# When the residual x and the small tables are loaded, and when the combinations of x are made

## The reference

```python
def swiglu(x, w_gate, w_up, w_down):
    return (jax.nn.silu(x @ w_gate) * (x @ w_up)) @ w_down

x = layer_norm(ALPHA * x + 0.5 * swiglu(x, ffn_w_gate[l, 0], ffn_w_up[l, 0], ffn_w_down[l, 0]), ln_g[l, 0], ln_b[l, 0])
```

## Time and profile before

| what | value |
|---|---|
| median of the runs | 1128.38 us (1127.18 to 1129.8) |
| the profiled execution's own time | 1126.32 us |
| its span, first to last instruction | 1124.3 us |
| PE busy | 1114.1 us, 99% |
| DVE busy | 776.9 us, 69% |
| ACT busy | 531.9 us, 47% |
| mean granted clock of PE | 0.999 |

### The profile page before, as it was taken

The page is one execution under the profiler, slowest core; times in us unless marked ns, Lnnn a source line. Parts: engine busy times, 40 slices in busy tenths (PEclk is TensorE's granted clock), DMA queues, the critical chain, the costliest instruction groups (busy, mean ns, idle before and its releaser), DMA issues.

```text
span 1124.3 us, 17750 instructions
## 1 busy us (share of the span) xinstructions
PE 1114.1 (99%) x6752; PEld 992.1 (88%) x6752; DVE 776.9 (69%) x1274; ACT 531.9 (47%) x913; POOL 35.5 (3%) x51
## 2 busy tenths in 40 slices
PE   9999999999999999999999999999999999999997
PEld 7899999988888888888898888889899999998886
DVE  4998898753338588774894865557898888863326
ACT  4555555543325477643463453436355555552222
POOL 2000000000002011000000000000000000000000
PEclk9999999999999999999999999999999999999999
DMA  8533333363222222342243242231233333353301
GB/s 286 201 113 113 107 101 111 96 211 94 94 75 89 80 77 84 104 150 75 75 157 126 88 156 75 73 97 58 75 127 99 113 113 96 113 185 99 108 21 75
DMA packets 34121, 123.37 MB, mean 110 GB/s; under 512 B 3916, under 2 KB 3932, under 8 KB 33792
## 3 DMA queue, kind: packets, MB, share of 16 engines
q1 hardware_dynamic: 30528, 109.07, 30.3%
q0 software_dynamic: 3520, 13.29, 3.5%
HBM read 120.23 MB, written 2.11 MB: 109 GB/s over the span
## 4 chain that ended last, share of the span: by engine, by line
PE 94%; DVE 3%; DMA 2%; ACT 1%; issue 0%; DVEq 0%; SPq 0%
PE ps L515 19%; PE ps L516 19%; PE ps L517 19%; PE ps L593 10%; PE ps L594 10%; PE ps L595 10%; DMA raw<-in_units 2%; PE ps L817 1%; PE ps L532 1%; PE ps L796 1%; PE ps L884 1%; PE ps L868 1%; PE ps L789 0%; PE ps L788 0%; PE ps L980 0%
## 5 line engine op out<-in xcount | busy, mean ns | idle before, releaser
L1572 DVE TENSOR_TENSOR wlo<-raw,whi 128x1024 fp32r<-128x1024 f32 x124 | 151.8, 1230 | 171.8 <-ACT whi L1046 170.8
L1046 ACT ACTIVATE whi<-raw 128x1024 fp32r<-128x1024 f32 (+1 forms) x131 | 134.4, 1033 | 135.3 <-PE ps L517 124.2
L515 PE MATMUL ps<-whi,hhi 128*128 128x512 f32 x480 | 187.9, 391 | 0.0
L517 PE MATMUL ps<-whi,hlo 128*128 128x512 f32 x480 | 186.9, 389 | 0.0
L516 PE MATMUL ps<-wlo,hhi 128*128 128x512 f32 x480 | 186.8, 389 | 0.0
L515 PE MATMUL ps<-xth,whi 128*128 128x512 f32 (+1 forms) x340 | 129.6, 381 | 0.0
L517 PE MATMUL ps<-xth,wlo 128*128 128x512 f32 (+1 forms) x340 | 127.5, 375 | 0.0
L516 PE MATMUL ps<-xtl,whi 128*128 128x512 f32 (+1 forms) x340 | 127.4, 375 | 0.0
L517 PEld LDWEIGHTS ps<-whi,hlo 128*128 128x128 f32 x480 | 90.1, 188 | 19.0
L515 PEld LDWEIGHTS ps<-whi,hhi 128*128 128x128 f32 x480 | 90.1, 188 | 18.5 <-ACT km L1046 0.3
L516 PEld LDWEIGHTS ps<-wlo,hhi 128*128 128x128 f32 x480 | 90.2, 188 | 17.9
(11 more groups left out here) (258 smaller groups left out, 2639.1 us busy)
## 6 DMA issues: line engine op xcount, KB each, us to landing
raw<-in_units SPq DMA_DIRECT2D x204, 512.0 KB, 3.5
xraw<-in_units POOLq DMA_DIRECT2D x1, 2048.0 KB, 13.3
xn<-in_x POOLq DMA_DIRECT2D x4, 512.0 KB, 15.2
gb<-in_ln_g POOLq DMA_DIRECT2D x4, 512.0 KB, 3.8
gb<-in_ln_b POOLq DMA_DIRECT2D x4, 512.0 KB, 5.3
wb<-in_bias_by_key POOLq DMA_DIRECT2D x8, 256.0 KB, 3.0
out<-xn SPq DMA_DIRECT2D x8, 256.0 KB, 2.1
gsp<-g_rows POOLq DMA_DIRECT2D x1, 1024.0 KB, 5.1
```

Source lines behind the costliest of these rows:

```text
L515: mm(dst, lh, rh, start=start, stop=False)
L517: return mm(dst, ll, rh, start=False, stop=stop)
L1046: return nc.scalar.activation(*a, **k)
L1572: v.tensor_tensor(wlo[c % SPL][:, :], raw[c % RAW][:, :], whi[c % SPL][:, :].bitcast(F32), ALU.subtract).then_inc(lo_done, 1)
```

## The change

On POOL a wait for `unit_used` is put between the load of `xraw` and the small tables. Its value is 4 + 8 + 2 = 14, which is reached when PE has done all of tile 4, `part4` included. On DVE and on ACT, for the first block alone (n is 0), tile 1 comes behind the combinations of x and not ahead of them.

```diff
--- before.py
+++ after.py
@@ -438,6 +438,7 @@
 
             pool.wait_ge(lo_done, KT - 2)
             pool.dma_start(xraw[0][:, :, :], units[0:KT, :, 0:S].rearrange("k p c -> p k c")).then_inc(xraw_in, 16)
+            pool.wait_ge(unit_used, U_F1 + 2 * FAST0 + 2)
             pool.dma_start(ccol[:, :], conv_cols).then_inc(small_in, 16)
             pool.dma_start(lnm_sb[:, :], lnm).then_inc(small_in, 16)
             pool.dma_start(gbias[:, 0:1], ig_bias.rearrange("a h -> h a")).then_inc(small_in, 16)
@@ -1163,10 +1164,13 @@
                         split(u0 + 2 * f + AHEAD + 1)
 
                 tile(0)
-                tile(1)
+                if n:
+                    tile(1)
                 for j, (x, rows, cols) in enumerate(((x5, high, far), (x7, low, far), (x6, low, near), (x3, high, near))):
                     act.wait_ge(xs_done, 4 * n + j + 1)
                     fn(x[n][0][:, :, :], xraw[n][:, rows, cols], ACT.Copy).then_inc(xc_hi_done, 1)
+                if n == 0:
+                    tile(1)
                 tile(2)
                 both, sums, last = fast_hi(n, FAST0)
                 both()
```

## The result

The changed kernel takes 1131.12 us (median of 12 runs, 1130.15 to 1132.52), the kernel before 1128.37 us (12 runs, 1127.01 to 1130.1). The ratio is 1.0024, with a 95% interval of 1.0016 to 1.0033: slower by 2.7 us, 1.8 to 3.7. The profiled execution took 1131.89 us, with a span of 1129.9 us and a mean granted clock of 0.997.

A forecast was written before the change was run, and what follows sets the result against it. PE was taken as the bound, busy 99%. A stop of 4.17 us and 0.1, less 1.96 regained, gave +2.3 us; on the median of 1128.38 that is 1130.7 us, range 1128.7 to 1134.3.

The forecast's parts named there:

- The stop at unit 10: Before tile 3 PE waits for unit 10's low part, behind the combinations on DVE: 4.17 us lost.
- What goes in return: PE's two waits in tile 4 (0.96 and 0.80 us) and their slow restarts go: 1.96 us back.
- The clock: At PE's stop before tile 3 the granted clock stays up; rival: it falls, +2.0 us, to 1132.7, chance 0.16.
- I am wrong if [...] the clock falls: Sign against the forecast: the granted clock, expected at 1.00 through 38 to 50 us, falls.
- The sum: By the start of tile 5: +4.17 + 0.1 - 1.96 = +2.3 us, which stays to the end.
- chance of 0.62 for slower: Chance that the whole kernel comes out slower by more than the 0.2% bound, 2.26 us; same 0.34, faster 0.04.
- Unit 11's low part: On DVE ahead of tile 3's second unit: 1.14 us later, still 5.4 us before PE wants it.
- The residual and the tables: Loads moved behind tile 4: put at 0, bounds 0 and +2.0 us; rival, they collide with weight loads, chance 0.10.
- the room that was worked out: In the fast tiles a weight load 2.0 us late would fit within 2.3 us of room before PE waits.
- The other side: Rival: not slower, the stop before tile 3 is worth less than the two waits removed; down to 1126.4, chance 0.08.

The follow-up runs named there:

- order alone: The changed kernel without POOL's wait, so residual and tables load as in the kernel before: 1130.56 us, ratio 1.0025 to the kernel before.
- splits first: The changed kernel with the high and low parts of units 10 and 11 ahead of the combinations: 1127.48 us, ratio 0.9996 to the kernel before.
- unit 10 in the middle: The changed kernel with unit 10's low part between the second and third low part of the combinations: 1127.67 us, ratio 0.9998 to the kernel before.
- short fill: The changed kernel with 8 identity matmuls into an unused bank where PE waits for unit 10: 1130.94 us, ratio 1.0025 to the kernel before.
- long fill: The changed kernel with 16 identity matmuls into an unused bank where PE waits for unit 10: 1129.45 us, ratio 1.0015 to the kernel before.
- unit 9 split early: The kernel before with late loads and ACT's high part of unit 9 ahead of its wait for the opening's end: 1126.65 us, ratio 0.9987.

## Why the prediction was right, and where its terms were not

- **The stop at unit 10.** Predicted 4.17 us with PE starting at 42.28; measured 4.18, at 42.67 (the opening ended 0.38 later in that execution, see below). The chain of its working (xraw in time, 9.45 us of combinations, ACT not in the way) stands in the rows one by one, and three experiments (order alone, splits first, unit 10 in the middle) move the time with the stop and with the waits and the clock that go with it.
- **What goes in return.** Both waits of tile 4 went. The size, 1.96 us, was that of the one execution I read. In two others it is 0.8 and 1.4 more by the waits. This term was too small, and what I took for fixed lengths hung on the landing of two loads, units 11 and 15.
- **The clock.** This is the step that failed, by the prediction's own sign ("I am wrong if [...] the clock falls"). I let it stay up, with a chance of 0.16 for a fall at +2.0. It fell in all three profiles with that stop (the changed kernel, the order alone, the short fill), and in the changed kernel the mean granted clock was 0.997 or less in each of the 12 executions. Its price is 1.6 us in the profile: some eight matmuls, each 0.2 us longer. The term of the prediction was nine, each 0.227 longer; no row that I predicted from shows a matmul at the lower clock, so the 0.227 was my estimate, from the fall to 0.50 in the earlier trace rows, where no matmul runs any more. The changed kernel shows starts 0.42 apart at 0.50. That price and the late end of the opening are why tile 5 began at 63.81 and not at 61.8. My reading, that a stop of 4.0 us would not lower it since the fall at the end of the kernel comes 4.2 us after PE's last matmul, failed: the 4.2 us were the figure of one execution (below).
- **The sum.** 4.2 + 1.6 less 1.96 less the 0.8 to 1.4 that other executions of before lose besides gives +2.4 to +3.0, and 2.7 was measured. Without the clock it gives +0.8 to +1.4; the long fill, which keeps the stop and not the fall, measured +1.7 (0.6 to 2.7). The terms are those of single executions, so this is agreement and no proof of each size. Two terms were thus wrong, by 1.6 and by 0.8 to 1.4 us, with opposite signs, and that the forecast of +2.3 came out so near is in part luck. The chance of 0.62 for slower was right in sign; with these rows it would have been higher.
- **Slips in the working.** Unit 11's low part, ready at 43.28 by that working, would be 4.4 us ahead of PE (47.7), not 5.4; and the chances as listed add up to 0.61 slower and 0.35 same, not 0.62 and 0.34. Neither moves the forecast.
- **The residual and the tables.** Put at 0, and no cost is shown (0.9996). The load of 9.8 us is no test of the room that was worked out: it was issued at 72.4 us and wanted at 84.4. The one that DVE waited for, issued behind `sbl` at 78.3, is: it landed 0.35 us late, within the 2.3.
- **The other side** had 0.08 and did not come.

The clock's step rests on those 4.2 us: PE is done at 1117.44, and the fall comes at about 1121.6. In the fourteen profiles of this study that time lies between 2.1 and 5.2 us, so it was no length that a stop has to exceed. The shortest is in the profile of unit 9 split early, where PE is done at 1117.0 (windows as above):

```profile
1116.75:1117.00 0.25, 0.24 (x2) 0.00 (x0) 0.00 (x0) 0.00 (x0) 0.00 (x0) 1.00 1.06 393
...
1119.00:1119.25 0.25, 0.00 (x0) 0.00 (x0) 0.25 (x1) 0.25 (x2) 0.00 (x0) 0.59 0.00 0
```

The two profiled executions, before and after, differ by 5.6 us and not by 2.7. By tile 5's start it is 4.31; 0.35 of that comes from the opening, whose first four matmuls of 512 columns took 1.63 us to the start of the next four (1.07 before) and began 0.21 earlier, and 1.3 from the attention. Both vary between executions of one kernel. A sum against one profile needs to know which of its waits are of that kind.

## What to carry to other kernels

Before work is moved ahead in an engine's list, look up what stands behind it there and when the bounding engine wants that: the price is the lateness of the first thing wanted, here one split of 1.2 us behind 9.45 us of work that was wanted more than ten us later. A wait that ends on a transfer had no fixed length here (unit 15's load took 3.7, 4.4 and 5.0 us in three profiles of one kernel), so profile the kernel before more than once and take the spread of such waits into the sum. And the stop of 4.0 us on TensorE was paid twice here, since the clock fell after it, for 1.6 us; it did not fall, in their profiles, behind the stop of 1.75 us, nor behind the one that small matmuls filled but for 0.45. So look at the granted clock behind a stop of the bounding engine, and measure it shorter or filled.

## What the runs showed that I had not expected

- In the four profiles with a fall the clock fell 1.1 to 1.5 us after PE had started again, not while it stood: in the changed kernel PE stopped at 38.65 and started at 42.67, the fall came at 44. A stop of 1.75 us left it at 1.00; a stop of 2.2 us behind 1.95 us of small matmuls lowered it; two waits of 1.09 and 1.77, nine us apart, did so in one execution of before, and two of about 1.15 in another did not. What decides it these runs don't show.
- The row of the granted clock reads 1.00 from the start of the kernel, but the first matmuls are slow: in the kernel before the eight of the identity's shape at 1.07 us (two records each) took 3.78 us, the eight at 38.65 in the short fill took 1.95. The four of 512 columns that come next take 0.99 to 1.84 us in the fourteen profiles, from their first start to the next four's, and these 0.91 to 0.93. So PE gains speed in the opening while the granted clock reads 1.00, and the time lost until then differs from execution to execution by up to 0.85 us. What slows it there these runs don't show.

```profile
1.07 3.78 PE L723 MATMUL ps<-eg 128*128 128x128 f32 x16 [1.07 <-DVE eg L1814]
```
